# Layer 1's modulation moves from layer 0's attention into the dense stage: fifteen weight chunks behind seven pairs of dense chunks, two in the norm's gap

## What is computed

```python
mod_x = jnp.split((cond_x @ w_mod[l] + b_mod[l])[:, None, :], 6, axis=-1)
mod_c = jnp.split((cond_c @ w_mod[l] + b_mod[l])[None, None, :], 6, axis=-1)
hx = modulate(rmsnorm(x, g_norm1[l]), mod_x[0], mod_x[1])
hc = modulate(rmsnorm(h_ctx, g_norm1[l]), mod_c[0], mod_c[1])
px = split_cols(hx @ w_in[l])
...
x = x + mod_x[2] * (jnp.concatenate([m_x, d_x, c_x], axis=-1) @ w_out[l])
...
x = x + mod_x[5] * ffn(modulate(rmsnorm(x, g_norm2[l]), mod_x[3], mod_x[4]))
```

## Time and profile before

| | |
|---|---|
| median of 3 runs | 1426.5 us (1424.1 to 1428.16) |
| the profiled execution's own time | 1426.68 us |
| its span in the trace | 1424.9 us |
| PE busy | 1376.9 us, 97% of the span |
| DVE, ACT, POOL busy | 975.6, 625.4, 188.4 us |
| mean granted TensorE clock | 0.987 of full |
| HBM traffic | 186 GB/s over the span |

### The profile page before, as it was taken

How to read it: one execution, slowest core, us unless ns; L and a number is a source line. 1 busy time by engine, 2 the same in 40 slices (tenths; PEclk the granted TensorE clock), 3 DMA queues, 4 the chain that set the end, 5 groups by cost and what they waited for, 6 DMA issues and landing times.

```text
span 1424.9 us, 20663 instructions
## 1 busy us (share of the span) xinstructions
PE 1376.9 (97%) x7798; PEld 1133.8 (80%) x7798; DVE 975.6 (68%) x1465; ACT 625.4 (44%) x988; POOL 188.4 (13%) x136
## 2 busy tenths in 40 slices
PE   7999999989999999999999989889999999999997
PEld 4788788567788888888878889587888888888886
DVE  3756787645743444353548697768898898898895
ACT  3434334551401100010016443656777777777774
POOL 0039980000000000000000991000000000000000
PEclk9999999979999999999999999999999999999998
DMA  9344443621422232222324222329978978978930
GB/s 396 142 180 177 178 178 119 243 113 66 151 109 89 91 116 89 89 93 92 111 106 175 89 89 90 118 80 404 399 300 316 358 295 319 353 298 319 349 144 30
DMA packets 30738, 265.51 MB, mean 186 GB/s; under 512 B 3408, under 2 KB 3536, under 8 KB 4944
## 3 DMA queue, kind: packets, MB, share of 16 engines
q1 hardware_dynamic: 30672, 264.58, 48.9%
HBM read 263.52 MB, written 1.05 MB: 186 GB/s over the span
## 4 chain that ended last, share of the span: by engine, by line
PE 86%; DVE 7%; ACT 3%; DMA 2%; issue 1%; SPq 0%; DVEq 0%; ACTq 0%
PE ps L552 38%; PE ps L1055 17%; PE ps L1075 9%; PE ps L889 4%; PE ps L574 3%; PE ps L1019 2%; PE ps L739 2%; DMA sb_arena<-mod 2%; PE ps L778 1%; PE ps L797 1%; PE ps L559 1%; DVE sb_h_lo L1623 1%; PE ps L788 1%; PE ps L704 1%; DVE sb_h_hi L1622 1%
## 5 line engine op out<-in xcount | busy, mean ns | idle before, releaser
L552 PE MATMUL ps<-sb_h_hi,sb_w_hi 128*128 128x512 f32 (+1 forms) x640 | 241.6, 378 | 2.4 <-DVE sb_w_lo L1623 1.2
L552 PE MATMUL ps<-sb_h_hi,sb_w_lo 128*128 128x512 f32 (+1 forms) x640 | 239.2, 374 | 0.0
L552 PE MATMUL ps<-sb_h_lo,sb_w_hi 128*128 128x512 f32 (+1 forms) x640 | 239.1, 374 | 0.0
L1055 PE MATMUL ps<-sb_egu_lo,sb_h_lo 128*128 128x512 f32 (+1 forms) x384 | 144.4, 376 | 0.0
L552 PEld LDWEIGHTS ps<-sb_h_hi,sb_w_hi 128*128 128x128 f32 x640 | 120.9, 189 | 28.2 <-DVE sb_w_lo L1623 2.1
L552 PEld LDWEIGHTS ps<-sb_h_hi,sb_w_lo 128*128 128x128 f32 x640 | 120.8, 189 | 21.6
L552 PEld LDWEIGHTS ps<-sb_h_lo,sb_w_hi 128*128 128x128 f32 x640 | 120.9, 189 | 20.6
L1622 DVE CAST sb_w_hi<-sb_arena 128x2048 fp32r<-128x2048 f32 (+1 forms) x38 | 45.5, 1196 | 129.3 <-PE ps L552 116.6
L2152 DVE TENSOR_TENSOR sb_ew_lo<-sb_arena,sb_ew_hi 128x1024 fp32r<-128x1024 f32 x88 | 107.4, 1220 | 12.8 <-ACT sb_ew_hi L1460 12.8
L2143 DVE TENSOR_TENSOR sb_egu_lo<-sb_arena,sb_con_r 128x1024 fp32r<-128x1024 f32 x96 | 113.6, 1218 | 1.2 <-ACT sb_con_r L1449 0.2
L1460 ACT ACTIVATE sb_ew_hi<-sb_arena 128x1024 fp32r<-128x1024 f32 x88 | 91.9, 1056 | 33.2 <-PE ps L1075 33.2
(11 more groups left out here) (346 smaller groups left out, 3013.1 us busy)
## 6 DMA issues: line engine op xcount, KB each, us to landing
sb_arena<-experts SPq DMA_DIRECT2D x89, 1536.0 KB, 8.6
sb_arena<-mod SPq DMA_DIRECT2D x48, 1024.0 KB, 4.9
sb_arena<-in SPq DMA_DIRECT2D x24, 1024.0 KB, 5.6
sb_arena<-gate SPq DMA_DIRECT2D x11, 1024.0 KB, 4.8
sb_arena<-up SPq DMA_DIRECT2D x11, 1024.0 KB, 4.7
sb_arena<-out SPq DMA_DIRECT2D x8, 1024.0 KB, 5.8
sb_arena<-down SPq DMA_DIRECT2D x8, 1024.0 KB, 4.8
sb_arena<-down SPq DMA_DIRECT2D x4, 768.0 KB, 4.1
```

What stands on the lines that cost most here:

```text
L552: ins = pe.matmul(o, left[a], right[b], start=(k == first and n == 0), stop=(k == final and n == len(PRODUCTS) - 1))
L1055: ins = pe.matmul(o, x[:, k, :], w[:, span, :], start=(k == 0 and n == 0), stop=(k == KD - 1 and n == 2))
```

## The change

The seven batches leave attention. Batch 0 takes the place of batch 14 in the norm's gap (two chunks instead of three). Batches 2, 4, ..., 14 go into the dense stage, one behind each of the pairs gate i, up i with i = 1 to 7; batch 14 has three chunks, and its turn now stands right behind it. On ACT the copies of the rows move along, each ahead of the silu of the next gate tile; on DVE the bias of chunks 0 to 13 moves from the end of attention to the end of the gate and up loop. The chunks' order in the ring changes in the same way. The amount of arithmetic is the same.

```diff
-MOD_ATTENTION = ((0, 2, 4, 6, 8, 10, 12), (20, 22))
-MOD_FILL = ((2, 4, 6, 8, 10, 12), (2,))
-MOD_NORM = {(0, 1): 14, (1, 0): 17}
-MOD_ENDS = ((0, 4), (0, 22), (1, 12))
+MOD_ATTENTION = ((), (20, 22))
+MOD_FILL = ((), (2,))
+MOD_NORM = {(0, 1): 0, (1, 0): 17}
+MOD_DENSE = {1: 2, 2: 4, 3: 6, 4: 8, 5: 10, 6: 12, 7: 14}
+MOD_ENDS = ((0, 4), (0, 22), (1, 14))
...
-                dense = [(k, 0, i) for i in range(FF // CHUNK) for k in ("gate", "up")]
+                dense = []
+                for i in range(FF // CHUNK):
+                    dense += [("gate", 0, i), ("up", 0, i)]
+                    if i in MOD_DENSE:
+                        dense += [("mod", 1, j) for j in batch(1, MOD_DENSE[i])]
...
                             ins.then_inc(*pe_done.tick((kind, 2 * i + m)))
+                    if i in MOD_DENSE:
+                        modulation(1, MOD_DENSE[i])
...
                 for i in range(FT):
+                    if i % 2 == 0 and i // 2 - 1 in MOD_DENSE:
+                        modulation_rows(1, MOD_DENSE[i // 2 - 1])
                     o = full(("gate", i))
...
                     split(("up", 0, i + 1) if i + 1 < FF // CHUNK else ("down", 0, (0, 1)))
+                modulation(1, 0, 28)
                 for f in range(UH + 2, FT):
...
                 attention(l)
-                if l == 0:
-                    modulation(1, 0, 28)
                 residual(l, "y", 16, lambda m: ("y", l, m))
```

## The result

The changed kernel takes 1438.3 us (median of 5 runs, 1436.5 to 1442.1) against 1426.5 us (5 runs): a ratio of 1.0084, 95% interval 1.0067 to 1.01, or 11.8 us more. The forecast was 1443.

What follows compares the result with a forecast made beforehand. PE was taken to bound the kernel, in attention and in the dense stage. Dense batches 20.6, wait 3.8, clock 1.5, less attention's 9.3, made +16.6 us: 1443 us against a median of 1426.5, range 1434 to 1455.

Steps and rivals of the forecast that it cites:

- the attention term: Layer 0's attention without its seven batches: shorter by 9.3 us net, after waits and clock loss.
- What was taken out, 18.3: PE time leaving attention: 14 chunks, 7 turns and the last turn's 0.50 us wait for ACT's copy, 18.3 us.
- Waits of 0.35 a unit over 16 units, 5.6: In attention's loop, new PE waits between closely matched engines take back 0.35 us a unit, 5.6 us lost.
- Extra half clock, 2.0 lost: In attention, PE idles earlier and oftener, so half clock (seen from 305.5 to 318.5) may start earlier: 2.0 us lost.
- Batches in the dense stage, forecast 20.6: In gate and up products, seven batches lie wholly on PE's path: 19.8 us plus 0.8 for slower first products.
- The wait behind up 7: Dense stage: gate 8's load waits for up 7, is ready 8.4 us after it; PE idles 3.8 us.
- The clock behind it: Behind the idle time after up 7, half clock costs PE 1.5 us.
- The norm's gap: Ahead of the dense stage, one chunk of three goes; products wait for DVE's splits, not PE: counted 0.
- Layer 1: All of layer 1 was to stay as before: counted 0.
- B: Rival: clock falls in attention, which gains nothing or loses up to 13 us; 1450 to 1466 us, chance 0.17.
- C: Rival: attention gives back 15.3 to 16 us, the wait behind up 7 leaves the clock up; 1431 to 1436, chance 0.11.
- E: Rival: the wait behind up 7 doesn't show, +11.3 us, 1438 us; chance 0.04.

Runs made afterwards that it cites:

- The seven pairs: Changed kernel with its three-chunk batch in the norm's gap and seven two-chunk batches in the dense stage: 1429.8 us, ratio 1.003.
- the three threes: Changed kernel with its fifteen dense-stage chunks cut into batches of 3, 3, 3, 2, 2, 1 and 1: 1454.5 us, ratio 1.0196.
- the fillers: Changed kernel with 8 spins (about 3.8 us of useless PE work) where PE idles behind up 7: 1437.0 us, ratio 1.0079.
- the run with one batch in the tail: Kernel before the change, with one modulation batch moved from attention step 12 to 16 and two output loads ahead of it: 1428.4 us, ratio 0.9996.
- seven-pair version with filler: The seven pairs kernel plus ten filler products in the idle places of layer 0's attention tail: 1431.5 us, ratio 1.0034.

## Why the prediction was right, and where its terms were off

The direction, the range and the mechanism hold: work that was partly hidden among waits went to a place where PE has none, and one chunk too many between two long ones made PE wait. The 4.7 us between 1443 and 1438.3 are the attention term, while four smaller misses cancel, which is luck.

- **Attention, forecast -9.3, measured -14.6.** Three parts of this term were off. What was taken out, 18.3, fits. The first batch gave back 0.6 (245.05 to 244.42), as counted 0.5. *Waits of 0.35 a unit over 16 units, 5.6*: between the transposes of unit 3 and unit 11, PE's row moved from 29.9 to 20.0 us (262.36 to 292.27, 258.82 to 278.79), 9.9 won; four batches of 2.54 and the last turn with its wait (1.04) are 11.2, so 1.3 was lost in 8 units, 0.16 a unit (by the windows PE idled for 1.7 us there, 0.21 a unit). I had taken a value from layer 1's rows between 0.1 and 0.99; the low end was the right one. In the tail, which had no batches before either, there was nothing to lose, and yet I counted its units. *Extra half clock, 2.0 lost*: the tail, from unit 11's transposes to the last sum of squares, went from 19.6 to 18.5 us, so it gained 1.1. Its mean clock was 0.81 against 0.74, by estimate 7 us at half clock instead of 10. The prediction also put the 1.65 us of wait at 296.51 right ahead of the half clock at 305.5; between them lay half clock from 298 to 302 us (mean 0.57) and a wait of 2.22 at 306.04. Only up to unit 3 did more get lost than I gave, about 2.2 of the 5.1 us of its two batches: PE waited twice for 0.79 us, and the clock was at half for some 3.4 us from 246 on. Lost altogether: 3.7 and not 9.0.
- **Batches in the dense stage, forecast 20.6, measured 21.6.** Two batches start 24.57 us apart (407.39, 431.96), two chunks take 21.76, so a batch costs 2.81 and six 16.9; I had 2.65 each. The rows at 407 say where 0.16 went: the batch starts 0.09 late, and the next products go at 0.24 instead of 0.23 for a while. The batch of three takes from 554.79 to 559.38 with its 0.50 us for ACT's copy, 4.6, as forecast, and 0.1.
- **The wait behind up 7, forecast 3.8, measured 4.09.** Each link is there: load issued at up 7's end, 5.0 to land, 3.6 to split, against 4.6 us of batch. The seven pairs show that it is the third chunk, and the three threes that it comes with each such chunk.
- **The clock behind it, forecast 1.5, measured 1.9** (gate 8 takes from 563.47 to 576.29, 12.82 us against 10.88), and 1.6 by the fillers, which leave the slower pace behind a batch where it is. The parts of this stage add up to 27.6, the table of stages gives 27.4.
- **The norm's gap, forecast 0, measured +0.9.** The spread took 2.07 us at half clock instead of 1.13, and DVE's splits behind it came that much later. The chunk that left isn't needed for it: with three chunks here the seven-pair version has the same spread (2.08). What made the clock fall is open, since the wait ahead of the sum of squares was as long as before (0.86 against 0.85).
- **Layer 1, forecast 0, measured -2.1** (-3.1 and +1.0). I had said that it would be as before, but the turn of batch 14, 0.54 us of PE's work, stood in its first norm and went to the dense stage, where I had counted it. The other 1.6 us are the clock's, and luck. The norm's half clock at 740 and the one at 845 did not come in the profile after; another came at 936. The sum of the terms was thus +27.4 + 0.9 - 14.6 - 2.1 = +11.6 where I had 25.9 - 9.3 = +16.6: the attention term missed by 5.3, and +1.5 in the dense stage, +0.9 and -2.1 nearly cancel.

Of the rivals, B (the clock falls early in attention) did not come as a loss of 10 us or more: both heads ran at 1.00 with idle times of up to 0.7 us. A short fall did come at attention's start (mean 0.91 from 242 to 260 us), but the run with one batch in the tail, whose first batch stands where it did, shows one too (0.59 from 248 to 252). The Trainium skill's rule ("TensorE: Matmul & The Clock Gate", Why this matters for your kernels), that TensorE falls back to half rate over long idle gaps, was no guide to this attention. The trace agrees with it behind up 7, where 4.09 us of idle time were followed by 0.50. In the tail half clock came after waits of 0.6 to 1.6 us with work between them; before the change the longest wait there was 2.22. The Trainium skill means longer gaps than these, so the rows at 305 were not the agreement that the prediction saw in them. C came near with its attention, 14.6 us of the 15.3 to 16 that it names, but not with its other condition: the wait behind up 7 did take the clock down. E's 1438 is the measured time, by coincidence: PE did stop behind up 7.

## What to carry to other kernels

Price work that is to move by the difference of two stages and not by its own duration: here a batch gave back 2.1 to 2.3 us where it stood and cost 2.8 where it went, so by these prices no division between the two stages wins. A ring of loads with a fixed depth takes only as many short chunks between long ones as leave the next long one time to load and be split; one chunk over it cost 7 of the 11.8 us, and a list of loads shows it before anything is run.
Where a filler product or a moved batch "wins" two or three microseconds by the clock, look at the next idle place and at ten runs before believing it.

## What the runs showed of the hardware that was not expected

- Half clock came after scattered short waits. In the tail of attention, PE was busy for 4.78 of 8 us from 282 to 290 at 1.00, with single waits of 1.6 us at most, and then ran at 0.52 for 14 us while it was busy for 11.56 of them. In layer 1 a stretch with less work held 1.00.
- Where a fall shows up differs from kernel to kernel, even among instructions that they share; that it also differs from run to run is inferred from the spread of times, since each kernel has one profile. The ten runs with one batch in the tail go from 1420.8 us at a mean granted clock of 0.990 to 1432.6 us at 0.984, for the same program on the same data. The Trainium skill ("TensorE: Matmul & The Clock Gate", What's actually happening) says that the number of slow products at a kernel's start varies between runs. The profiles here agree for the first 40 us, which are the same program in all kernels: the mean clock is 0.96 in the kernel before and 0.91 in the seven-pair version with filler. In the middle of the program layer 1's first norm had 0.71 before the change and 1.00 after it. What decides at which idle place it falls stays open.
- One load of 1 MB (gate 4 in the run with three batches of three) took 6.5 us where the two gate loads before it took 4.9, with the same loads issued behind it. Why is open.
